# Second feed-forward part: another order of the 256 values within each matmul

## The chip, the cores and the metric

One core of a Trainium2 chip runs the whole kernel. The metric is the device time in microseconds (us) of one execution; lower is better.

## The reference

Two transformer blocks with D_MODEL 2048 on 256 tokens, in float32. Around the change, in the second block, the reference computes:

```python
def conv_gated_mlp(h, w_up, conv_w, conv_b, w_down):
    gate, up = jnp.split(h @ w_up, 2, axis=-1)
    return (jax.nn.gelu(dwconv_centred(gate, conv_w, conv_b), approximate=True) * up) @ w_down
...
        x = x + g2 * conv_gated_mlp(modulate(rmsnorm(x, norm2_g[l]), sh2, sc2), *ffn)
...
    return rmsnorm(x, final_norm_g)
```

w_up is 2048 x 11264 and w_down 5632 x 2048. What comes before (the first block, with attention, spatial gating and its own feed-forward; the modulation; the second block's attention, Fourier and long-convolution mixing) isn't touched by the change.

## The kernel before

**Chunks.** All weights go through TensorE in chunks of 512 x 512. A chunk c is loaded by SyncE's queue (1 MB, `load`, L347) into one of four buffers RAW, then split by halves into a high part WH (ScalarE, L519) and a rest WL (VectorE, L981), each with two buffers. The activations are split the same way into high and low (XH, XL; HH, HL). TensorE forms high x high, high x low and low x high, so a float32 product takes three matmuls in the format fp32r. The 400 chunks in which the weights are the stationary operand go through `ws` (L1786): per chunk 4 blocks kk of 128 rows x 4 blocks f of 128 columns x 3 products = 48 matmuls on line 1791. Each has a 128x128 block of weights as stationary operand and one activation tile of 128 partitions x 256 tokens as moving operand, and adds to `out[:, f, :]`, 256 columns of PSUM (two f share a bank of 512). A few earlier chunks go through `tok` (L1796), where the weights are the moving operand, 512 columns wide (L1802, L1804, L1805).

**Steps of the second feed-forward.** There are STEPS2 = 11 steps of 512 hidden columns. The part begins with 8 chunks (gate and up of step 0, numbers C_FF2 to C_FF2 + 7). Then `ff2_step(j)` (L2191) for j = 0 to 9, 12 chunks each: the gate of step j + 1 (4 chunks, `wide`), its up (4, `wide`), and the down product of step j (4, `down`). The last 4 chunks are the down product of step 10. Together 132 chunks. `wide` reads 16 tiles of XH and XL, `down` 4 tiles of HH and HL. In SBUF a tile is 1024 bytes per partition. With the base of 16512 bytes (L161), XH, XL, HH and HL begin at a multiple of 64 bytes; the first two tiles of XH are kept apart as XH_FIRST (L178, `tile_of` L207), which begins 32 bytes past a multiple of 64. In a `wide` of 4 chunks the first chunk reads XH_FIRST in 16 of its 48 matmuls.

**The engines beside it.** VectorE and ScalarE do, beside the splitting, the depthwise convolution (L1697 to L1707), gelu, the gating (L1715), the split of the hidden tile (L937, L1353) and the addition to X (L1720). Each engine's order is written out by hand and is the same for every step; they are tied by semaphores. TensorE waits for each half chunk's WH and WL (`high_ready`, `low_ready`), and for a free accumulator (`use`); two accumulators of two banks each take turns. After the last chunk come the last addition, the root of the mean square, the final norm and the output.

**Where the code decides.** `ws` is called from `product` (L1808), which passes the chunk's place c; in this part c.base is a constant for every chunk, since the steps are written out and not looped.

Of the kernel before, what the change touches and what calls it, by code (L numbers as in the profile page):

```python
# [8 lines left out]
P = 128  # L9
# [35 lines left out]
STEP1, STEP2 = 2 * SLOTS, 3 * SLOTS  # L45
# [9 lines left out]
C_FF2 = C_OUT2 + 4 * SLOTS  # L55
# [100 lines left out]
def build_program(nc, d, out):  # L156
# [6 lines left out]
    with ExitStack() as ctx:  # L163
# [126 lines left out]
        def acc_ws(s):  # L290
            return PS[:, 2 * s:2 * s + 2, :].rearrange("p b (h t) -> p (b h) t", t=T)
# [4 lines left out]
        def bank(n):  # L296
            return PS[:, n, :]
# [4 lines left out]
        def ctx_ws(n):  # L302
            return ctx_as(n).rearrange("p b (h t) -> p (b h) t", t=T)
# [42 lines left out]
        def _(sp):  # L346
# [77 lines left out]
            def ff1_step(j, first=False):  # L424

                c, _, a = ff1_place(j)
                order = Place(8 * j.base, j.i, 8 * j.per)
                for s in range(STEP1):
                    if s < SLOTS:
                        load(c.plus(s), cut(w_ff1, s, j.value(NB, NB)))  # L430
                    else:
                        load(c.plus(s), w_ff2[j.value()][:, :, (s - 4) * NB:(s - 3) * NB])
                    if s >= 2:
                        load_piece(a, s - 2, order.plus(s - 2))
                    elif not first:
                        load_piece(a.plus(-1), s + 6, order.plus(s - 2))
# [532 lines left out]
        def _(dve):  # L969
# [57 lines left out]
            def split_low(e, hi, lo, src, n):  # L1027
                dve.wait_ge(x_hi, 4 * e + n + 1)
                for (l4, k), (h4, _) in zip(parts_of(lo, n), parts_of(hi, n)):
                    ins = tt(l4, src[:, k, :], h4.bitcast(f32), ALU.subtract)  # L1030
                ins.then_inc(x_lo, 1)
# [740 lines left out]
        def _(pe):  # L1772
            MM = nc.tensor.matmul
# [7 lines left out]
            def use(q):  # L1781

                if q.since(2):
                    pe.wait_ge(acc_free[q.slot], q.turns(2))

            def ws(out, c, xh, xl, first, last, kk, low):  # L1786

                b = c.base % 2
                for n, (w, x) in enumerate(((WL, xh),) if low else ((WH, xh), (WH, xl))):
                    for f in (0, 2, 1, 3):  # L1790
                        ins = MM(out[:, f, :], w[:, b, kk, f * P:(f + 1) * P], x,  # L1791
                                 start=first and not low and n == 0 and f % 2 == 0, stop=last and low,
                                 skip_group_check=True)
                return ins
# [13 lines left out]
            def product(c, q, s, xh, xl, k0=0, first=True, last=True, fn=ws, out=None, e=None):  # L1808

                if q is not None and first:
                    use(q)
                early = s == 0 and e in WINDOWS
                if early:
                    pe.wait_ge(first_lo, WINDOWS.index(e) + 1)
                elif e is not None:
                    pe.wait_ge(x_lo, 4 * e + s + 1)
                if out is None:
                    out = (acc_ws if fn is ws else acc_as)(q.slot)
                for h in range(2):  # L1820
                    high_ready(c, h)
                    if h and early:
                        pe.wait_ge(x_lo, 4 * e + 1)
                    for low in (False, True):
                        if low:
                            low_ready(c, h)
                        for kk in range(HF * h, HF * h + HF):
                            ins = fn(out, c, tile_of(xh, k0 + kk), tile_of(xl, k0 + kk), first and kk == 0,
                                     last and kk == FT - 1, kk, low)
                    ins.then_inc(pe_half, 1)  # L1830

            def wide(c, q, s, fn=ws, e=None, xh=XH, xl=XL):

                product(c, q, s, xh, xl, 4 * s, s == 0, s == SLOTS - 1, fn, e=e)
# [92 lines left out]
            for c in range(C_OAB):  # L1927
                if c == 4:
                    pe.wait_ge(sm["mats_in"], 16)
                    norm_sum(N_IN, NT)  # L1930
                if T_SGU <= c < T_SGU + 8 and (c - T_SGU) % 2 == 0:
                    spatial_gating((c - T_SGU) // 2)
                if T_QK < c < T_QK + 16 and (c - T_QK) % 4 == 1:
                    head_sums((c - T_QK) // 4)
                for h in range(HEADS):
                    attention_step(h, c - T_ATT - S_ATT * h)
                first_columns(c)
                g, s = divmod(c, SLOTS)
                wide(Place(c), Place(g), s, tok if 4 <= g < 8 else ws,
                     {0: E_GAIN1, 2: E_NORM1}.get(g))  # L1940

            for n in range(4):
                for s in range(SLOTS):
                    c = Place(C_OAB + 4 * n + s)
# [3 lines left out]
                    if s == 2 and n >= 2:  # L1948
                        pe.wait_ge(sm["b_free"], n - 1)
                    product(c, Place(Q_OAB + n) if s < 2 else None, s, XH, XL, 4 * s, s % 2 == 0, s % 2 == 1,  # L1950
                            out=acc_ws((Q_OAB + n) % 2) if s < 2 else ctx_ws(n), e=E_OAB)
# [36 lines left out]
            c, q = Place(C_FF1_TAIL), Place(Q_FF1_TAIL)  # L1988
# [66 lines left out]
            for t in range(10 * SLOTS):  # L2055
                n, s = divmod(t, SLOTS)
# [31 lines left out]
            for n in range(FNG):  # L2088
# [3 lines left out]
                for m in range(2):  # L2092
                    ins = MM(bank(6 + n % 2)[:, 0:T], fcd[:, m, :], fU[:, n, m * T:(m + 1) * T],
                             start=m == 0, stop=m == 1)
# [212 lines left out]
```

## Time and profile before

| | us |
|---|---|
| median of 2 runs | 2567.72 (2567.47 to 2567.96) |
| the profiled execution | 2575.35 |
| its span, first to last instruction | 2573.6 |
| TensorE busy with matmuls | 2550.8 |
| VectorE busy | 1930.8 |
| ScalarE busy | 1140.4 |
| mean granted TensorE clock | 0.996 |

The rows below come from that one profiled execution. Matmuls are pipelined, so their durations overlap and a busy TensorE is not TensorE at its peak; the distance between starts tells the rate. PE is TensorE, PEld its weight load, DVE VectorE, ACT ScalarE, L1791 line 1791.

### The profile page before, as it was taken

What the parts mean: (1) busy time and instruction counts of PE and PEld (TensorE: products, weight loads), DVE (VectorE), ACT (ScalarE), POOL (GpSimd) and SP (SyncE); (2) the same over time, 40 slices, a digit from 0 to 9 for tenths busy, and PEclk for the clock granted to TensorE, in tenths of its full rate; (3) what the DMA queues carried; (4) which work ended last, traced back from release to release, by engine and by line L of the source; (5) the groups of instructions that cost most, each with busy time, mean ns of one, the idle gap of its engine ahead of it and who ended that gap; (6) DMA issues with size and microseconds to landing.
All of it is one profiled execution on the core that took longest, in us unless ns stands there. A gap on an engine that the chain in (4) does not pass through costs nothing.

```text
span 2573.6 us, 49600 instructions
## 1 busy us (share of the span) xinstructions
PE 2550.8 (99%) x20808; PEld 2468.6 (96%) x20808; DVE 1930.8 (75%) x2468; ACT 1140.4 (44%) x1225; POOL 0.2 (0%) x4
## 2 busy tenths in 40 slices
PE   9999999999999999999999999999999999999998
PEld 9889999999999999999999899959999999999998
DVE  8978887997999888888893237777766666666667
ACT  6556554444544444444442234333444444444443
POOL 0000000000000000000000000000000000000000
PEclk9999999999999999999999999989999999999999
DMA  8766767767888888888863254424555555555553
GB/s 312 259 238 214 241 230 249 249 240 247 289 285 286 290 283 285 287 284 284 280 234 104 94 180 148 143 76 152 169 190 196 197 192 190 193 196 197 190 190 113
DMA packets 282441, 558.10 MB, mean 217 GB/s; under 512 B 10295, under 2 KB 16728, under 8 KB 281944
## 3 DMA queue, kind: packets, MB, share of 16 engines
q1 hardware_dynamic: 282120, 553.47, 64.1%
q8 instruction: 133, 2.18, 0.3%
q10 hardware_dynamic: 144, 2.10, 0.2%
q14 instruction: 44, 0.36, 0.0%
HBM read 553.43 MB, written 2.10 MB: 216 GB/s over the span
## 4 chain that ended last, share of the span: by engine, by line
PE 93%; DVE 4%; DMA 1%; issue 1%; ACT 1%; SPq 0%; DVEq 0%; ACTq 0%
PE PS L1791 80%; PE PS L1805 3%; PE PS L1802 3%; PE PS L1804 3%; DVE WL L981 1%; PE PS L2123 1%; DMA w3h<-in_hy_w 1%; DMA adab<-in_ada_w 0%; PE PS L2038 0%; DMA X<-in_x 0%; PE PS L2112 0%; PE PS L1869 0%; DVE ada1c L1240 0%; DVE SQ L1007 0%; PE PS L2133 0%
## 5 line engine op out<-in xcount | busy, mean ns | idle before, releaser
L519 ACT ACTIVATE WH<-RAW 128x1024 fp32r<-128x1024 f32 x840 | 889.3, 1061 | 1278.2 <-PE PS L1791 1151.6
L981 DVE TENSOR_TENSOR WL<-RAW,WH 128x1024 fp32r<-128x1024 f32 x840 | 1018.1, 1223 | 579.7 <-ACT WH L519 570.6
L1791 PE MATMUL PS<-XL,WH 128*128 128x256 f32 x4288 | 664.2, 277 | 0.0
L1791 PE MATMUL PS<-XH,WH 128*128 128x256 f32 x3752 | 585.9, 278 | 1.6 <-ACT WH L519 0.9
L1791 PEld LDWEIGHTS PS<-XL,WH 128*128 128x128 f32 x4288 | 569.1, 188 | 0.0
L1791 PE MATMUL PS<-XH,WL 128*128 128x256 f32 x3752 | 503.2, 276 | 0.0
L1791 PEld LDWEIGHTS PS<-XH,WH 128*128 128x128 f32 x3752 | 498.2, 188 | 3.9 <-issue 2.3
L1791 PEld LDWEIGHTS PS<-XH,WL 128*128 128x128 f32 x3752 | 461.5, 188 | 0.0
L1791 PE MATMUL PS<-HH,WH 128*128 128x256 f32 x1728 | 268.0, 277 | 1.5 <-DVE X L1359 1.5
L1791 PE MATMUL PS<-HL,WH 128*128 128x256 f32 x1728 | 266.2, 276 | 0.0
L1791 PE MATMUL PS<-HH,WL 128*128 128x256 f32 x1728 | 231.1, 276 | 0.0
L1791 PEld LDWEIGHTS PS<-HH,WH 128*128 128x128 f32 x1728 | 228.3, 188 | 2.0 <-DVE X L1359 1.9
L1791 PEld LDWEIGHTS PS<-HL,WH 128*128 128x128 f32 x1728 | 228.0, 188 | 0.0
L1791 PEld LDWEIGHTS PS<-HH,WL 128*128 128x128 f32 x1728 | 212.0, 188 | 0.0
L1240 DVE SCALAR_TENSOR_TENSOR ada1c<-ada1b,ctmp,ada1c 128x512 f32<-128x512 f32 x240 | 164.3, 746 | 0.1
L1398 DVE SCALAR_TENSOR_TENSOR adac<-adab,ctmp,adac 128x512 f32<-128x512 f32 x224 | 157.3, 745 | 1.6 <-DMA adab<-in_ada_w 1.5
L1805 PE MATMUL PS<-WH,XL 128*128 128x512 f32 x224 | 87.9, 392 | 0.0
L1791 PE MATMUL PS<-XH_FIRST,WH 128*128 128x256 f32 x536 | 86.1, 283 | 0.0
L1359 DVE TENSOR_TENSOR X<-PS,X 128x1024 f32<-128x1024 f32 x64 | 77.9, 1217 | 0.0
L1804 PE MATMUL PS<-WH,XH 128*128 128x512 f32 x196 | 77.8, 397 | 0.0
L1791 PE MATMUL PS<-XH_FIRST,WL 128*128 128x256 f32 x536 | 73.6, 280 | 0.0
L1720 DVE SCALAR_TENSOR_TENSOR X<-PS,mod,X 128x256 f32<-128x256 f32 x176 | 72.7, 476 | 0.0
(278 smaller groups left out, 1848.4 us busy)
## 6 DMA issues: line engine op xcount, KB each, us to landing
RAW<-in_w_ff SPq DMA_DIRECT2D x128, 1024.0 KB, 6.2
RAW<-in_w_in SPq DMA_DIRECT2D x111, 1024.0 KB, 5.2
RAW<-in_w_up SPq DMA_DIRECT2D x88, 1024.0 KB, 5.0
adab<-in_ada_w SPq DMA_DIRECT2D x128, 512.0 KB, 5.4
RAW<-in_w_down SPq DMA_DIRECT2D x44, 1024.0 KB, 5.0
ada1b<-in_ada_w SPq DMA_DIRECT2D x64, 512.0 KB, 6.1
RAW<-in_w_out SPq DMA_DIRECT2D x32, 1024.0 KB, 5.1
RAW<-in_w_oa SPq DMA_DIRECT2D x8, 1024.0 KB, 5.2
```

The costliest lines, as they stand in the source:

```text
L519: A(WH[:, c.base % 2, hs], RAW[:, c.base % SLOTS, hs], ACT.Copy).then_inc(hi_done, 1)
L981: tt(WL[:, b, hs], RAW[:, c.base % SLOTS, hs], WH[:, b, hs].bitcast(f32), ALU.subtract)\
L1240: stt(acc, w, x, acc, ALU.mult, ALU.add)
L1359: tt(quarter(X, s), acc_ws(q.slot), quarter(X, s), ALU.add).then_inc(acc_free[q.slot], 1)
L1398: ins = ts(acc, w, x, None, ALU.mult) if n == 0 else stt(acc, w, x, acc, ALU.mult, ALU.add)
L1720: ins = stt(X[:, 4 * s + k, :], acc_ws(q.slot)[:, k, :], mod[:, 5 * KC + 4 * s + k, 0:1], X[:, 4 * s + k, :], ALU.mult, ALU.add)
L1791: ins = MM(out[:, f, :], w[:, b, kk, f * P:(f + 1) * P], x, start=first and not low and n == 0 and f % 2 == 0, stop=last and low, skip_gro ...
L1802: ins = MM(out[:, t, :], h, WL[:, b, kk, :], start=False, stop=last)
L1804: MM(out[:, t, :], h, WH[:, b, kk, :], start=first, stop=False)
L1805: ins = MM(out[:, t, :], l, WH[:, b, kk, :], start=False, stop=False)
L2123: ins = MM(bank(n % 2), Ef[:, 5 * t + m, :], hSD[:, o, 1 if m in (2, 3) else 0, t, :], start=t == 0, stop=t == 1)
```

## The change

`ws` passes both its output and its moving operand through `walked`, which gives the same 256 values in another order, as one access pattern with three dimensions. n is the number of the 12-chunk group, counted from the first chunk of the part; for chunks ahead of the part n is negative and the order stays plain, and so it does for n = 0 and n = 10. Group n begins at the up of step n: 4 up chunks and the 4 down chunks of `ff2_step(n - 1)`, then the 4 gate chunks of `ff2_step(n)`.

```diff
+            LINES = [(), ("t", 2, 16), ("h", 2, 16), ("t", 2, 32), ("h", 2, 2), ("t", 2, 2),
+                     ("t", 2, 8), ("t", 4, 16), ("h", 4, 16), ("h", 2, 4), ()]
+
+            def walked(x, c):
+
+                n = (c.base - C_FF2) // STEP2
+                if n < 0 or not LINES[n]:
+                    return x
+                kind, b, w = LINES[n]
+                if kind == "r":
+                    return x.rearrange("p (a w) -> p a w", w=w)[:, ::-1, :]
+                if kind == "t":
+                    return x.rearrange("p (a b w) -> p b a w", b=b, w=w)
+                return x.rearrange("p (b a w) -> p a b w", b=b, w=w)
+
             def ws(out, c, xh, xl, first, last, kk, low):
...
-                        ins = MM(out[:, f, :], w[:, b, kk, f * P:(f + 1) * P], x,
+                        ins = MM(walked(out[:, f, :], c), w[:, b, kk, f * P:(f + 1) * P], walked(x, c),
                                  start=first and not low and n == 0 and f % 2 == 0, stop=last and low,
                                  skip_group_check=True)
```

"t", b, w: pieces of w values; first every b-th piece from piece 0, then every b-th from piece 1, and so on. With ("t", 2, 16): values 0 to 15, 32 to 47, ..., then 16 to 31, 48 to 63, .... "h", b, w: the tile is cut in b parts, and pieces of w values are taken from the parts in turn. With ("h", 2, 2): values 0, 1, 128, 129, 2, 3, 130, 131, .... A value has 4 bytes, so a piece of 16 is 64 bytes and one of 2 is 8 bytes. Kind "r" isn't used.

## Rows read from the trace of the kernel before

**Rows 1.** The page: span, TensorE's share, the chain by engine and line.

```profile
span 2573.6 us, 49600 instructions
...
PE 2550.8 (99%) x20808; PEld 2468.6 (96%) x20808; DVE 1930.8 (75%) x2468; ACT 1140.4 (44%) x1225; POOL 0.2 (0%) x4
...
PE 93%; DVE 4%; DMA 1%; issue 1%; ACT 1%; SPq 0%; DVEq 0%; ACTq 0%
PE PS L1791 80%; PE PS L1805 3%; PE PS L1802 3%; PE PS L1804 3%; DVE WL L981 1%; PE PS L2123 1%; DMA w3h<-in_hy_w 1%; DMA adab<-in_ada_w 0%; PE PS L2038 0%; DMA X<-in_x 0%; PE PS L2112 0%; PE PS L1869 0%; DVE ada1c L1240 0%; DVE SQ L1007 0%
```

**Rows 2.** The nine changed groups by window: busy us, count, clock, DMA share.

```profile
core 0: us, PE busy (x) PEld busy (x) DVE busy (x) ACT busy (x) POOL busy (x), PEclk, DMA share, GB/s
1903.98:1969.49 65.51, 65.51 (x579) 65.51 (x577) 42.40 (x55) 28.30 (x27) 0.00 (x0) 1.00 0.58 193
...
2428.04:2493.54 65.50, 65.50 (x578) 65.50 (x577) 42.40 (x55) 28.30 (x27) 0.00 (x0) 1.00 0.59 194
sum 589.56, PE 589.56 PEld 589.56 DVE 381.65 ACT 254.73 POOL 0.00; mean PE 65.51 PEld 65.51 DVE 42.41 ACT 28.30 POOL 0.00
```

**Rows 3.** The chain of waits within the nine groups.

```profile
by line: PE PS L1791 100.0%
...
1903.92 589.67 PE PS L1791 x5185
```

**Rows 4.** All waits in the nine groups: waiting <- waited for: us, times, longest.

```profile
ACT WH L519 <- PE PS L1791: 334.8, 216, 1.8
DVE WL L981 <- ACT WH L519: 205.5, 153, 1.6
```

**Rows 5.** Groups of instructions by shape within the nine groups.

```profile
L1791 PE MATMUL PS<-XL,WH 128*128 128x256 f32 x1152 | 178.0, 277 | 0.0
...
L1791 PEld LDWEIGHTS PS<-XL,WH 128*128 128x128 f32 x1152 | 152.5, 188 | 0.0
...
L1791 PE MATMUL PS<-HH,WH 128*128 128x256 f32 x576 | 88.7, 276 | 0.0
...
L1791 PE MATMUL PS<-XH_FIRST,WH 128*128 128x256 f32 x144 | 22.7, 280 | 0.0
```

**Rows 6.** Timeline of TensorE over one down chunk (start us, us, what, xcount).

```profile
1996.80 0.62 PE L1791 MATMUL PS<-HH,WH 128*128 128x256 f32 x4
...
2002.24 0.62 PE L1791 MATMUL PS<-HH,WH 128*128 128x256 f32 x4
```

**Rows 7.** Timeline of TensorE, matmuls 512 columns wide.

```profile
133.17 0.39 PE L1804 MATMUL PS<-WH,XH 128*128 128x512 f32 x1
...
135.91 0.39 PE L1804 MATMUL PS<-WH,XH 128*128 128x512 f32 x1
```

**Rows 8.** Timeline of TensorE, a chunk that begins with XH_FIRST.

```profile
2493.54 0.63 PE L1791 MATMUL PS<-XH_FIRST,WH 128*128 128x256 f32 x4
...
2496.36 0.63 PE L1791 MATMUL PS<-XH,WH 128*128 128x256 f32 x4
2496.83 0.62 PE L1791 MATMUL PS<-XL,WH 128*128 128x256 f32 x4
...
2499.09 0.62 PE L1791 MATMUL PS<-XH,WH 128*128 128x256 f32 x4
```

**Rows 9.** Timeline of TensorE, a chunk with XH_FIRST in the slower gait.

```profile
465.08 0.63 PE L1791 MATMUL PS<-XH_FIRST,WH 128*128 128x256 f32 x4
465.55 0.63 PE L1791 MATMUL PS<-XL,WH 128*128 128x256 f32 x4
...
467.89 0.63 PE L1791 MATMUL PS<-XH,WH 128*128 128x256 f32 x4
...
470.72 0.63 PE L1791 MATMUL PS<-XH,WH 128*128 128x256 f32 x4
```

**Rows 10.** Timeline of TensorE, matmuls of plain 4-byte numbers.

```profile
1832.67 5.34 PE L1922 MATMUL PS<-mats 128*128 128x256 f32 x24
1837.66 0.58 PE L1791 MATMUL PS<-XH_FIRST,WH 128*128 128x256 f32 x2
```

## The prediction

> **What bounds the kernel now.** I read the shares and the chain first. TensorE is busy for 2550.8 of 2573.6 us and the chain of waits that ended last lies on it for 93%, 80% on line 1791 alone, which is the line that changes [rows 1]. Then I cut the part of the second feed-forward where another order applies into its nine groups of 12 chunks. A group is 12 chunks x 48 matmuls = 576; the nine are 5184 matmuls and take 589.56 us, 65.51 us each, at a granted clock of 1.00, the upper level of 2.4 GHz [rows 2]. In this stretch the chain is one piece of line 1791 [rows 3], and nobody makes TensorE wait: the waits are ScalarE's for TensorE (334.8 us) and VectorE's for ScalarE (205.5 us) [rows 4]. VectorE works 42.41 and ScalarE 28.30 us of each 65.51, the transfers have a share of 0.58 [rows 2]. So the time of this stretch is the number of matmuls times the spacing of their starts, and a slower matmul has no cover at all: each nanosecond on each of the 5184 is 5.18 us of the total.
>
> **The spacing.** A matmul's row says 276 ns [rows 5], but they overlap; the starts tell the rate. Down chunks: from 1996.80 to 2002.24 us, 48 matmuls, 5.44 us, 113.3 ns each [rows 6]. 256 columns at 2.4 GHz are 106.7 ns, 256 cycles; 113.3 ns are 272 cycles, 16 too many, which is one for each 16 values or 64 bytes of the tile read. The matmuls 512 columns wide, 12 of them from 133.17 to 135.91 us, start 228 ns apart [rows 7], so the extra goes with the columns and isn't a fixed cost of an instruction. Whether reading, writing or the weight load (188 ns in its rows, overlapped [rows 5]) makes it, no row tells.
>
> **The change part by part.** No instruction, wait, buffer or transfer is added, removed or moved. What changes is the order in which one matmul walks its 256 values: it reads x in pieces and writes the sums in the same pieces, so value t still goes to place t. Accumulation over the matmuls is as before. Chunks 0 to 11 and 120 to 131 of the part keep the plain order; nine groups get the orders of LINES. Per matmul I count two things. Breaks in the run of addresses: 16, 16, 8, 128, 128, 32, 16, 16, 64 for groups 1 to 9, together 424. And changes of the 64-byte piece being read (the plain order has 16): 16, 16, 16, 128, 32, 32, 16, 16, 64, together 336, which is 192 more than the 144 of nine plain orders. (XH_FIRST lies 32 bytes off, so that its pieces of 16 and 32 straddle one boundary more; that is 32 matmuls of a group's 576 and left out of the counts.)
>
> *Reading.* The trace of before has no broken order, so I bound it by the nearest rows. From below: the spacing can't go under 106.7 ns; if a new order took all extra cycles away, 5184 x 6.7 ns = 34.6 us would go. Nothing tells that a detour over other pieces would remove a cycle per 64 bytes, and the weight load beside it may want the same time. From above: the nearest row in which a matmul's reading lies otherwise on the addresses is XH_FIRST, which by its offset begins 32 bytes off the 64-byte grid, while XH, XL, HH and HL begin on it. Its matmuls stand at 280 ns beside 276 [rows 5], and the chunk that has 16 of them takes from 2493.54 to 2499.09, 5.55 us [rows 8], 0.11 us more than a plain one. That is 7 ns for each misaligned matmul, some 17 cycles, and such a matmul touches 17 pieces instead of 16. One reading of this is that each touched piece costs its full 17 cycles however little of it is used; then groups with 2, 4 or 8 values per piece would pay 192 x 7.08 ns x 576 = 783 us. The rows speak against it: in the stretch from 465.08 us all matmuls start 117.7 ns apart, aligned or not; 24 with the 16 misaligned ones take 465.08 to 467.89 (2.81 us), the next 24, all aligned, 467.89 to 470.72 (2.83 us) [rows 9]. Four misaligned ones there take 0.47 us (465.08 to 465.55), 117.5 ns each, while 17 x 17 cycles would be 120.4. And after the misaligned ones of 2493.54 the first aligned four still go at 117.5 (2496.36 to 2496.83) [rows 8]: it is a slower gait of the engine, which something small sets off. I take this as the price of a disturbance: 4.4 ns x 5184 = 23 us if all of the changed matmuls fell into it. 
>
> *Writing.* The same breaks hit the accumulation. The nearest rows for an engine at a slower rate are those of line 1922, 256 columns of plain 4-byte numbers: 24 of them from 1832.67 to 1837.66, 0.208 us each [rows 10], about two cycles per column. That is the price if every write (or read) went alone. I take nothing here too, by the same reason.
>
> The Trainium skill says two things of this. Its page "Advanced Engine Details and Errata", section Memory Cachelines, says that every two consecutive values in PSUM should be contiguous for best throughput, and that a 16-byte line of SBUF wants at least two hits; all nine orders keep both, and by it the sum stays at nothing. The same section and "PSUM — Partial Sum Buffer", section Specifications (TRN2), also say that any non-contiguous pattern in PSUM slows matmuls significantly; by that all nine groups would be slow, which is the third rival below. No row of this trace shows either, as none has a broken pattern.
>
> *The engines beside it.* If the spacing grows, VectorE and ScalarE, which have 23.1 and 37.2 us to spare in each group [rows 2], get more, and the loads more time. Nothing new can become late. After the last chunk the tail is untouched.
>
> **The sum.** Profiled execution: 2575.35 us, its span 2573.6. The changed stretch stays at 589.56 us, all others stay. The median of the runs is 7.6 us under the profiled one, so I apply differences to the median: 2567.72 + 0 = 2567.7. A measurement of this kernel tells about 2%, 51.4 us, from no change: 9.9 ns on each changed matmul.
>
> **The rivals.**
> 1. *The cycle per 64 bytes is a cycle per change of piece.* For: 16 extra cycles for 16 pieces, 32 for the wide ones [rows 6, 7]. Against: it may as well be a beat of time. Price: 192 x 0.417 ns = 80 ns over the nine orders, x 576 = 46 us: 2613.8. It shows in h 2 2 (+47 ns), h 2 4 (+20), t 2 2 and t 2 8 (+7 each).
> 2. *Slower: every break of the run costs.* Place: TensorE's walk over addresses, on line 1791 in groups 1 to 9. With one cycle of 2.4 GHz per break: 424 x 0.417 ns x 576 = 101.8 us: 2669.5. With two (one at 1.2 GHz): 203.6 us: 2771.3. For: there is no cover, and two of the nine orders break every 2 values. Against: nothing but that pairs may be the unit. It decides (over 2%) from 0.21 ns per break. A doubling of only the two groups of 2 values, 2 x 65.5 = 131 us, 2698.7, lies within it.
> 3. *Every broken pattern goes at the rate of one value at a time.* 208 - 113.7 = 94 ns x 5184 = 489 us: 3057. For: the engine has such a rate [rows 10], and one mechanism, writes that are gathered only along an unbroken run, would put all nine orders on it. Against: a pair is whole in every order, and those rows are of another number format, which by itself may be the cause. (This is the form that the Trainium skill's "PSUM — Partial Sum Buffer", section Specifications (TRN2), gives to the matter; no row here bears it out.)
> 4. *The detour saves the extra cycles*: up to 34.6 us less: 2533.
>
> **How the numbers follow.** No effect, or one within a disturbance of the gait: 0.50. Rival 1: 0.12. Rival 2: 0.27. Rival 3: 0.08. Rival 4: 0.03. The likeliest gives 2567.7, its own range 2550 (half of rival 4) to 2591 (all at 117.7 ns). The range reaches to rivals 1 and 2: 2545 to 2771; rival 3, the whole of 4 and still dearer breaks stay out, some 0.15. Slower by over 2%: rivals 2 and 3 and the upper quarter of rival 1, 0.38. Faster by over 2% could come only with more than rival 4 gives: 0.01. Within 2%: 0.61.
>
> **What would show it.** Right: all nine groups still take 65.5 us, chunks without XH_FIRST 5.44 us. Rival 1: only groups 4, 5, 6 and 9 grow, and 4 far more than 5, though both break every two values. Rival 2: groups 4 and 5 grow alike, by 31 us or more, and the groups of 16 values by 4 us. Rival 3: all nine at about 120 us. If ScalarE's waits for TensorE grow by what the groups grow, the time is TensorE's own; if TensorE shows waits before line 1791, my reading that nobody holds it was wrong. The prediction is wrong if pieces of 2 or 4 values alone cost more than 51 us.

## The result and the profile after

The changed kernel takes 2693.59 us (median of 2 runs, 2692.77 to 2694.41) against 2567.72; the ratio on record is 1.0488, 95% interval 1.0471 to 1.0505. It is slower by 125.9 us. That is inside the range of the prediction and not what it called likeliest.

The page of the changed kernel, which answers to [rows 1]; line 1806 is now the matmul of `ws`:

```profile
span 2691.0 us, 49600 instructions
...
PE 2669.6 (99%) x20808; PEld 2579.3 (96%) x20808; DVE 1931.9 (72%) x2468; ACT 1140.5 (42%) x1225; POOL 0.2 (0%) x4
...
PE 93%; DVE 4%; DMA 1%; issue 1%; ACT 1%; SPq 0%; DVEq 0%; ACTq 0%
```

The count of instructions is the same and so is the work of VectorE and ScalarE; only TensorE, with its weight load, is busy for longer. The two spans, 2691.0 and 2573.6 us, differ by only 117.4 us because the profiled execution of before had lost 8.5 us ahead of the part: its first chunk starts at 1837.66 us, that of the changed kernel at 1829.18. Its granted clock was 0.92 from 1650 to 1700 us and 0.94 from 1700 to 1750, where the changed kernel had 1.00. Here are the nine groups by window, as in [rows 2] (length and busy us of each engine, then the granted clock, the share of the transfers and GB/s):

```profile
1895.81:1965.70 69.89, 69.89 (x579) 69.89 (x578) 42.52 (x55) 28.23 (x27) 0.00 (x0) 1.00 0.56 183
1965.70:2034.86 69.16, 69.16 (x578) 69.16 (x577) 42.50 (x55) 28.32 (x27) 0.00 (x0) 1.00 0.55 183
2034.86:2104.00 69.14, 69.14 (x579) 69.14 (x578) 42.50 (x55) 28.28 (x27) 0.00 (x0) 1.00 0.56 183
2104.00:2198.77 94.77, 94.77 (x579) 94.77 (x578) 42.59 (x55) 28.20 (x27) 0.00 (x0) 1.00 0.43 139
2198.77:2330.84 132.07, 132.07 (x577) 119.68 (x577) 42.59 (x55) 28.19 (x27) 0.00 (x0) 1.00 0.29 96
2330.84:2399.86 69.02, 69.02 (x577) 69.02 (x576) 42.52 (x55) 28.29 (x27) 0.00 (x0) 1.00 0.54 177
2399.86:2468.90 69.04, 69.04 (x579) 69.04 (x577) 42.51 (x55) 28.26 (x27) 0.00 (x0) 1.00 0.55 183
2468.90:2537.93 69.03, 69.03 (x579) 69.03 (x578) 42.52 (x55) 28.25 (x27) 0.00 (x0) 1.00 0.55 184
2537.93:2610.95 73.02, 73.02 (x578) 73.02 (x577) 42.51 (x55) 28.84 (x27) 0.00 (x0) 1.00 0.53 176
sum 715.14, PE 715.14 PEld 702.75 DVE 382.76 ACT 254.86 POOL 0.00; mean PE 79.46 PEld 78.08 DVE 42.53 ACT 28.32 POOL 0.00
```

715.14 less 589.56 of before is 125.6 us: the whole difference lies in the nine groups. Divided by 576, one matmul costs, against 113.7 ns before:

| group, order | ns | us over before |
|---|---|---|
| 1: t 2 16 | 121.3 | 4.4 |
| 2: h 2 16 | 120.1 | 3.7 |
| 3: t 2 32 | 120.0 | 3.6 |
| 4: h 2 2 | 164.5 | 29.3 |
| 5: t 2 2 | 229.3 | 66.6 |
| 6: t 2 8 | 119.8 | 3.5 |
| 7: t 4 16 | 119.9 | 3.5 |
| 8: h 4 16 | 119.8 | 3.5 |
| 9: h 2 4 | 126.8 | 7.5 |

The two orders of 2 values hold 95.9 us, three quarters. The waits and the chain in these groups (they answer to [rows 3, 4]):

```profile
ACT WH L519 <- PE PS L1806: 460.0, 216, 4.5
DVE WL L981 <- ACT WH L519: 327.5, 181, 4.3
```
```profile
1895.75 715.24 PE PS L1806 x5185
```

ScalarE's wait for TensorE grew by 125.2 us, from 334.8 to 460.0, as much as the groups; TensorE still waits for nobody. In group 5 the starts of four matmuls are 0.92 us apart, where it was 0.45:

```profile
2250.12 1.10 PE L1806 MATMUL PS<-HH,WH 128*128 128x256 f32 x4
2251.04 1.10 PE L1806 MATMUL PS<-HL,WH 128*128 128x256 f32 x4
```

So the time is TensorE's own. What the profile doesn't tell is which side of a matmul it is: the reading of the tile from SBUF, or the adding in PSUM.

### The profile page after: what moved, and what is told of

It reads as the page before. It is cut to its first block, busy times and chain, and to the rows that moved or that the text cites. A ratio compares the mean times of both kernels' runs of the same rounds, so it can differ in the third digit from the quotient of the medians.

```text
span 2691.0 us, 49600 instructions
## 1 busy us (share of the span) xinstructions
PE 2669.6 (99%) x20808; PEld 2579.3 (96%) x20808; DVE 1931.9 (72%) x2468; ACT 1140.5 (42%) x1225; POOL 0.2 (0%) x4
## 4 chain that ended last, share of the span: by engine, by line
PE 93%; DVE 4%; DMA 1%; issue 1%; ACT 1%; SPq 0%; DVEq 0%; ACTq 0%
PE PS L1806 81%; PE PS L1817 2%; PE PS L1820 2%; PE PS L1819 2%; DVE WL L981 1%; PE PS L2138 1%; DMA w3h<-in_hy_w 0%; PE PS L2053 0%; DMA X<-in_x 0%; DVE ada1c L1240 0%; DVE X L1359 0%; PE PS L1884 0%; DVE SQ L1007 0%; DVE NT L1023 0%; PE PS L2148 0%
## 5 line engine op out<-in xcount | busy, mean ns | idle before, releaser
L1806 PE MATMUL PS<-XL,WH 128*128 128x256 f32 x4288 | 692.7, 284 | 0.0
L1806 PE MATMUL PS<-XH,WH 128*128 128x256 f32 x3752 | 611.0, 285 | 2.4 <-ACT WH L519 1.5
L1806 PEld LDWEIGHTS PS<-XL,WH 128*128 128x128 f32 x4288 | 588.9, 189 | 2.8
L1806 PE MATMUL PS<-XH,WL 128*128 128x256 f32 x3752 | 528.3, 284 | 0.0
L1806 PEld LDWEIGHTS PS<-XH,WH 128*128 128x128 f32 x3752 | 515.8, 189 | 7.1 <-issue 2.9
L1806 PEld LDWEIGHTS PS<-XH,WL 128*128 128x128 f32 x3752 | 481.6, 189 | 2.4
L1806 PE MATMUL PS<-HH,WH 128*128 128x256 f32 x1728 | 282.6, 286 | 0.3 <-DVE X L1359 0.3
L1806 PE MATMUL PS<-HL,WH 128*128 128x256 f32 x1728 | 280.8, 285 | 0.0
L1806 PE MATMUL PS<-HH,WL 128*128 128x256 f32 x1728 | 245.5, 285 | 0.0
L1806 PEld LDWEIGHTS PS<-HL,WH 128*128 128x128 f32 x1728 | 238.3, 189 | 1.4
L1240 DVE SCALAR_TENSOR_TENSOR ada1c<-ada1b,ctmp,ada1c 128x512 f32<-128x512 f32 x240 | 164.5, 748 | 0.1
L1806 PEld LDWEIGHTS PS<-XH_FIRST,WH 128*128 128x128 f32 x536 | 74.6, 189 | 0.6
```

The source lines that it names most:

```text
L1240: stt(acc, w, x, acc, ALU.mult, ALU.add)
L1806: ins = MM(walked(out[:, f, :], c), w[:, b, kk, f * P:(f + 1) * P], walked(x, c), start=first and not low and n == 0 and f % 2 == 0, stop= ...
```

## The experiments

In all of them a group is one of the nine, 576 matmuls long, and a window of one divided by 576 is the spacing. Groups are named by number and order.

Seven of the runs (reads alone, writes alone, more orders, single values, shifted starts, wider matmuls, the weights' addresses) are one execution each; what they tell is read from their windows, in which a group with the same code repeats within 0.05 us from run to run, but for the slower gait told of below. `order` is `walked` with its table given from outside, and g is the number of the group. All diffs are against the kernel before.

**Reads alone, writes alone.** Two kernels with the nine orders on one operand, READS or WRITES, and the plain order on the other:

```diff
-                        ins = MM(out[:, f, :], w[:, b, kk, f * P:(f + 1) * P], x,
+                        ins = MM(order(out[:, f, :], WRITES[g]), w[:, b, kk, f * P:(f + 1) * P], order(x, READS[g]),
```

> The reads follow the nine orders, the writes keep the plain order, so each matmul adds the token columns to other places than it should: the output of the second feed-forward is shuffled, the amount of work is the same. In the changed kernel the spacing of the starts per group was 121.3, 120.0, 120.0, 164.4, 229.3, 120.0, 120.0, 120.0, 126.7 ns (plain 113.3). Theory R (the reading of the tile from SBUF is the limit): all nine spacings as in the changed kernel within 1 ns, time about 2693 us. Theory W (the writing to PSUM is the limit): all nine at 113.3 ns plus the 0.4 ns of XH_FIRST, time about 2568 us. Theory B (the constant step to 120 ns comes from one side, the growth with pieces of 2 and 4 values from the other): groups 4, 5 and 9 differ from the changed kernel and the six others don't, or the other way round.

> The writes follow the nine orders, the reads keep the plain order (the output of the second feed-forward is shuffled, the work is the same). Theory R (reading is the limit): all groups at 113.7 ns, time about 2568 us. Theory W (writing is the limit): spacings 121.3, 120.0, 120.0, 164.4, 229.3, 120.0, 120.0, 120.0, 126.7 ns, time about 2693 us. Theory B (each side has a share): what is missing in the run with the reads alone stands here.

Measured: 2696.1 us with the reads alone, 2568.5 us with the writes alone, beside 2567.4 for the kernel before. Windows of groups 1, 4, 5 and 9 of the first (busy us of TensorE, clock, share of transfers, GB/s):

```profile
1899.16:1969.04 69.88, 69.88 (x578) 1.00 0.56 184
...
2107.34:2202.11 94.77, 94.77 (x578) 1.00 0.41 139
2202.11:2334.19 132.08, 132.08 (x579) 1.00 0.29 96
...
2541.27:2614.30 73.03, 73.03 (x579) 1.00 0.53 175
```

and groups 4 and 5 of the second:

```profile
2093.65:2159.15 65.50, 65.50 (x578) 1.00 0.58 193
2159.15:2224.66 65.51, 65.51 (x579) 1.00 0.58 193
```

This is theory R: all of the cost is in the reading, to 0.01 us per group. Beside a reading at 113.7 ns none shows in the writing, not even with pairs from two halves of the block. The 2.5 us by which the reads alone are over the changed kernel lie ahead of the groups: group 1 begins at 1899.16 instead of 1895.81.

**Without the two orders of 2 values.** Groups 4 and 5 plain, the rest as in the change:

```diff
+            READS = [(), ("t", 2, 16), ("h", 2, 16), ("t", 2, 32), (), (), ("t", 2, 8), ("t", 4, 16), ("h", 4, 16), ("h", 2, 4), ()]
+            WRITES = [(), ("t", 2, 16), ("h", 2, 16), ("t", 2, 32), (), (), ("t", 2, 8), ("t", 4, 16), ("h", 4, 16), ("h", 2, 4), ()]
```

> The change without the two orders of 2 values (groups 4 and 5 are plain, the seven others as in the change). By the groups of the changed kernel these two hold 29.3 and 66.6 us of the 125.5 us, so if the groups are independent and TensorE alone sets the time: 2693.6 - 95.9 = 2597.7 us, 1.2% over the kernel before. Rival: the cost is one of the clock or of a wait that the slow groups hand on to later ones; then groups 6 and 9 change too and the time is off by more than 5 us.

Measured: 2597.97 us, ratio to before 1.0119 (1.0103 to 1.0134). The costs of the groups add up, but for one detail. Groups 4 and 5, both plain now:

```profile
2105.21:2172.30 67.09, 67.09 (x579) 1.00 0.57 186
2172.30:2237.80 65.50, 65.50 (x578) 1.00 0.59 194
```

Group 4 takes 1.6 us more than the same code in group 5. It is in a slower gait, a spacing of some 117.8 ns that lasts over many matmuls, which the prediction had seen near 465 us [rows 9]. Group 4 cut at the second of its two chunks that begin with XH_FIRST:

```profile
2105.21:2150.43 45.22, 45.22 (x387) 1.00 0.57 186
2150.43:2153.71 3.28, 3.28 (x30) 1.00 0.44 166
2153.71:2172.30 18.59, 18.59 (x167) 1.00 0.60 191
```

The first 8 chunks, after the broken order of group 3, take 117.8 ns per matmul (45.22 us for 384), though the first of them begins with XH_FIRST; the 28 matmuls from 2150.43 take 117.1; the rest, 164 matmuls, 113.4.

**XH_FIRST on the grid of 64 bytes, and off it at another place.** The kernel before with one offset changed:

```diff
-        XH_FIRST = at("XH_FIRST", [P, 2, T], 80 * K + 32, f32r)
+        XH_FIRST = at("XH_FIRST", [P, 2, T], 80 * K + 64, f32r)
```

> The kernel before, with XH_FIRST moved from 32 to 64 bytes past its old origin, so that it begins on a multiple of 64 bytes; plain order everywhere. If the 0.11 us that each chunk with XH_FIRST costs comes from its place: these chunks take 5.44 us instead of 5.55 in the two feed-forwards (36 of them and about 12 elsewhere), 48 x 0.113 = 5.4 us less, 2562 us. If it comes from something else at the start of a wide product (a semaphore wait, the change of the accumulator): 5.55 us as before and no difference.

Measured: 2624.82 us, ratio 1.0222 (1.0209 to 1.0236), so both sides of the expectation were wrong. The first of its nine groups, all of which take 67.82 or 67.83 us (117.8 ns per matmul):

```profile
1931.23:1999.06 67.83, 67.83 (x579) 1.00 0.56 186
```

With 96 instead of 64:

> The kernel before with XH_FIRST 96 bytes past its origin instead of 32: again 32 bytes off the grid of 64, but at another place. The run with XH_FIRST on the grid was 57 us slower, with all matmuls at 117.8 ns instead of 113.3. Theory G (a tile that begins off the grid pushes reading and weight loading back into the faster of two gaits): as before, 2567 us, 113.3 ns in most chunks. Theory A (the distance between addresses decides by itself, the grid has no part): some other share of slow chunks, a time anywhere between 2567 and 2625 us.

Measured: 2566.55 us, ratio 0.9993 (0.9983 to 1.0003), groups at 65.52 us. This agrees with theory G, as far as three places can tell: two tiles off the grid, which I had read as a small loss (0.11 us per chunk, [rows 8]), keep most of the kernel in the faster gait; on the grid the nine groups go at 117.8 ns. They hold 21 of the 57 us; some 34 lie ahead of group 1, which begins at 1931.23 us instead of 1896.90 (run with more orders). That a chunk with XH_FIRST ends the slower gait is seen in group 4 of the run without the two orders of 2 values, at 2153.71 us, but not each of them does: the one at 2105.21 there didn't, and neither did the one at 465.08 us in the kernel before [rows 9]. What decides it stays open.

**More orders.** Both operands in one order again, WRITES with the same table as READS:

```diff
+            READS = [(), ("t", 2, 64), ("h", 2, 64), ("h", 2, 32), ("t", 2, 4), ("t", 4, 2), ("h", 4, 2), ("t", 8, 2), ("t", 4, 4), ("h", 2, 8), ()]
```

> Nine other orders, for reads and writes, in groups 1 to 9: t 2 64, h 2 64, h 2 32, t 2 4, t 4 2, h 4 2, t 8 2, t 4 4, h 2 8. Theory L: the reader fetches 16 bytes at a time (four values) and one such fetch costs 4.25 to 4.75 cycles of 2.4 GHz, whatever part of it is used. Plain: 64 fetches, 113.3 ns. So t 2 64, h 2 64, h 2 32, h 2 8: 120 ns; t 2 4 and t 4 4: 120 to 127 ns; t 4 2 and t 8 2: 128 fetches, 229 ns as t 2 2; h 4 2 like h 2 2 if a fetch is kept for a moment, else 229. Theory N: the price of t 2 2 comes from going to the next neighbour; with pairs 32 or 64 bytes apart (t 4 2, t 8 2) it falls to the 164 ns of h 2 2 or less. Theory C: the price is one per break (424 breaks of the change); then t 2 64 and h 2 64 with 4 breaks stand at 113 to 115 ns, not 120.

Measured: 113.7, 113.7, 118.8, 117.8, 233.3, 223.4, 219.9, 114.5, 123.3 ns. Windows of groups 1, 4, 5, 7 and 8:

```profile
1896.90:1962.41 65.51, 65.51 (x579) 1.00 0.58 193
...
2096.36:2164.21 67.85, 67.85 (x579) 1.00 0.56 187
2164.21:2298.57 134.36, 134.36 (x578) 1.00 0.30 98
...
2427.25:2553.91 126.66, 126.66 (x578) 1.00 0.30 100
2553.91:2619.84 65.93, 65.93 (x577) 1.00 0.56 183
```

Pairs 32 or 64 bytes apart (t 4 2, t 8 2) and pairs from four parts in turn (h 4 2) cost about the double as well, so theory N falls. Theory L was right on the pairs, but wanted 120 ns for pieces of 64 and got 113.7. Pieces of 4 with 64 breaks cost 114.5 ns and pieces of 64 nothing, so the price isn't one per break either, though t 2 64 came out as theory C had it. And a pattern of three dimensions by itself is free.

**Single values, and more writes.**

```diff
+            READS = [(), ("t", 2, 1), ("t", 4, 1), ("h", 2, 1), ("t", 16, 1), ("t", 16, 2), ("t", 16, 4), (), (), (), ()]
+            WRITES = [(), (), (), (), (), (), (), ("t", 16, 2), ("h", 16, 2), ("h", 16, 4), ()]
```

> Groups 1 to 6 read t 2 1, t 4 1, h 2 1, t 16 1, t 16 2, t 16 4 and write plainly; groups 7 to 9 read plainly and write t 16 2, h 16 2, h 16 4 (so the output of the second feed-forward is shuffled, the work is the same). Theory L (a fetch of 16 bytes costs 4.25 to 4.75 cycles): t 2 1 has two values of each fetch, 229 ns; t 4 1 and t 16 1 one value, 256 fetches, about 459 ns; t 16 2 229 ns; t 16 4 about 127 ns; h 2 1 alternates between two lines and shows whether two fetches are kept: 120 to 130 ns if so, 459 if not. Rival (two hits in a 16-byte line are enough, the slow orders suffer from something else): t 2 1 at 113 to 120 ns. Writes: 113.7 ns in groups 7 to 9 if the writing order is free for pieces of two values or more; 120 ns or more if strides of 64 bytes matter there.

Measured: 229.3, 233.3, 111.7, 220.0, 228.4, 135.3 ns, then 113.7 three times for the writes. Groups 1 to 3:

```profile
1897.29:2029.36 132.07, 132.07 (x578) 1.00 0.30 101
2029.36:2163.76 134.40, 134.40 (x578) 1.00 0.28 94
2163.76:2228.09 64.33, 64.33 (x577) 1.00 0.57 186
```

Theory L falls: t 4 1 takes one value from each 16 bytes and should have cost 459 ns, it costs 233, no more than two values from each. And h 2 1, which breaks after every single value, is the fastest of all, faster than plain. What both have in common becomes visible if the order is cut in twos and the first and the second place of each two are followed apart (the even and the odd places). In h 2 1 the even places read 0, 1, 2, 3 and the odd ones 128, 129, 130, 131, each staying in its line of 16 bytes for four values. In t 2 1, t 2 2, t 4 1 and t 16 2 each stream changes its line with every value. In pieces of 4 on a line's start it has two values per line. This is theory S, put to the test next. The three orders of the writes are free too; writes of single values were not run, so nothing tells what they cost.

**Shifted starts.** Each matmul reads 256 values from an offset within two tiles:

```diff
+                    read = two.rearrange("p k t -> p (k t)")[:, kind[0]:kind[0] + T]
+                    if len(kind) > 1:
+                        read = order(read, *kind[1:])
```

> Groups 1 to 9 read 256 values that begin 2, 4, 8, 12 values after the start of an even tile (plain order), then from 2 on as t 2 4, from 2 on as t 2 8, then from 0 on as h 4 1 and h 8 1, and from 8 on as h 2 1; writes plain, the products are not the right ones, the amount is. Theory S: the reader takes the values by twos, the even and the odd places of the order each from a 16-byte line that serves only as long as the next value of that stream lies in it; a line that serves one place alone costs double, one that serves two is free. So pieces of 4 at a distance of 2 values from the line's start (t 2 4 from 2) cut each line in one pair each: 220 to 233 ns, while the same order from 0 took 117.8; t 2 8 from 2: between the two, about 170 ns; h 4 1: its even places alternate between two lines like h 2 2: 150 to 230 ns; h 8 1: 220 to 233; h 2 1 from 8: 111.7. Rival P (what counts is the length of the piece, 4 or more is nearly free wherever it begins): t 2 4 and t 2 8 from 2 at 114 to 127 ns. The plain order from 2, 4, 8, 12: all 113 to 120 ns in both; those off the grid of 64 bytes (all four are) at 117 to 120 if being off the grid is what costs XH_FIRST its time.

Measured: 120.0, 116.8, 118.3, 117.3 ns for the plain order from 2, 4, 8, 12. Then t 2 4 from 2: 229.9. t 2 8 from 2: 166.7. h 4 1: 143.3. h 8 1: 220.1. h 2 1 from 8: 111.7. Groups 5 to 9:

```profile
2171.00:2303.43 132.43, 132.43 (x579) 1.00 0.30 100
2303.43:2399.47 96.04, 96.04 (x577) 1.00 0.40 132
2399.47:2482.01 82.54, 82.54 (x578) 1.00 0.46 153
2482.01:2608.80 126.79, 126.79 (x578) 1.00 0.30 100
2608.80:2673.14 64.34, 64.34 (x578) 1.00 0.57 187
```

The same pieces of four cost 117.8 ns from 0 and 229.9 from 2. This tells the two theories apart: it isn't the length of the piece but how it lies on the lines of 16 bytes. t 2 8 from 2 has pairs alone in their line for two of its four twos, and costs half of the doubling, as worked out ahead. h 4 1 at 143 ns is a little under its bound. There and in h 2 2 (164.5) each stream alternates between two lines and pays a part of the doubling; where it goes through four lines in turn (h 8 1, 220.1; h 4 2, 223.4) it pays nearly the whole, which theory S as it stands doesn't explain. In every order that was run the even and the odd places change their line at the same twos, so whether the two streams really count apart, or a two of places counts as one access, isn't told.

**Wider matmuls, patterns that only go upward.** Groups 1 to 5 read two tiles with 512 columns, groups 6 to 9 every other piece of two tiles:

```diff
+                            read = order(two, *kind[1:]) if len(kind) > 1 else two
+                            write = out[:, f:f + 2, :].rearrange("p f t -> p (f t)")
+                        else:
+                            read = two.rearrange("p (a b w) -> p b a w", b=2, w=kind[1])[:, k % 2]
```

> The products of groups 1 to 9 are not the right ones here, the amount read and added is. Groups 1 to 5: matmuls of 512 columns that read two tiles in one and write two blocks (half as many matmuls): plain, t 2 16, t 2 2, h 2 2, h 2 4. Groups 6 to 9: 256 columns, every other piece of 128, 16, 4, 2 values out of two tiles, a pattern of two dimensions that goes upward only; writes plain. If the extra goes with the columns: 226.7, 240, 459, 329, 253 ns for the 512-wide ones, and it is the reading; if the step from 113.3 to 120 is a fixed cost of an instruction with a broken pattern: t 2 16 at 233 ns. If it is the weight load (128 columns, the same for either width) that holds the spacing at 113.3: plain at 213 to 220 ns. Groups 6 to 9: if any break brings the step, 120 ns already for half 128 (one break), else 113.3; half 16: 120; half 4: 120 to 127; half 2: 128 fetches of 16 bytes, 229 ns.

Measured, per matmul of 512 columns (288 to a group): 233.1, 238.3, 453.3, 326.7, 252.3 ns. Half 128, 16, 4, 2: 116.5, 121.7, 117.5, 229.9 ns. Groups 1, 3, 4 and 9:

```profile
1899.64:1966.76 67.12, 67.12 (x291) 1.00 0.57 188
...
2035.40:2165.95 130.55, 130.55 (x289) 1.00 0.30 100
2165.95:2260.05 94.10, 94.10 (x290) 1.00 0.41 134
...
2537.61:2670.02 132.41, 132.41 (x579) 1.00 0.30 100
```

The dear orders double with the columns though the weight load is the same 128 columns, so it is the tile's reading that makes them. The plain 512 columns stand at 233.1 ns and not at the 213 to 220 of a spacing that the weight load holds. Of the patterns that only go upward, half 2 came out as expected (229.9) and half 4 below its 120 to 127. Half 128 came out between the two values that were named: part of that group goes in the faster gait, the larger part in the slower.

**The weights' addresses.** The tile plain in groups 1 to 6 and t 2 16 in 7 to 9:

```diff
+                            o = f // 2 * P + WEIGHTS[g][0]
+                            block = w[:, b, kk, o:o + P]
+                            if len(WEIGHTS[g]) > 1:
+                                block = w[:, b, kk, 0:P * WEIGHTS[g][1]:WEIGHTS[g][1]]
```

> The tile is read in plain order in groups 1 to 6 and as t 2 16 in 7 to 9; what changes is the block of weights that each matmul loads (so the products are not the right ones, the amount is the same): from 0, 4, 8, 16 values past a block's start in groups 1 to 4, every second and every fourth value in groups 5 and 6, from 0, 8, 16 in groups 7 to 9. Theory I (the small differences, 113.3 against 117.8 in plain order and the step to 120 with pieces of 8 to 32, come from tile reading and weight loading meeting in the same memory, so they hang on how their addresses lie to each other): the groups 1 to 4 differ by 1 ns or more among themselves, and so do 7 to 9; groups 5 and 6, where the weights come from two and four times as many lines, go slower by several ns or more. Theory T (the tile's own reading makes them all): 113.3 (or 117.8 where the engine is in its slower gait) in groups 1 to 6 and 121.3 as before in 7 to 9, whatever the weights do.

Measured: 113.7, 118.6, 117.5, 118.6 ns with the weights from 0, 4, 8, 16; 120.1 and 233.3 with every second and every fourth value; 121.3, 120.1, 120.1 for t 2 16. Groups 1, 2 and 6:

```profile
1895.73:1961.24 65.51, 65.51 (x578) 1.00 0.58 193
1961.24:2029.55 68.31, 68.31 (x579) 1.00 0.57 187
...
2234.70:2369.10 134.40, 134.40 (x579) 1.00 0.30 98
```

Theory I's condition is met: with the same tile in the same order, 16 bytes more in the weights' address cost 4.9 ns, and groups 7 to 9 differ by 1.2. So the weights' address bears on the small differences; that the two meet in the same memory is only argued. A weight load with one value per 16 bytes brings the spacing to 233.3 ns beside a plain tile.

**A version that beats both.** h 2 1 on the reads of the second feed-forward, with plain writes; the sums then stand in another order of tokens, and their three readers put them back (the gating, in four instructions instead of one, is left out here):

```diff
+                                 x.rearrange("p (b a) -> p a b", b=2) if c.base >= C_FF2 and c.i is None else x,
...
+                A(GS[:, :, :].rearrange("p k (b a) -> p k a b", b=2),
+                  acc_ws(q.slot).rearrange("p k (a b) -> p k a b", b=2), ACT.Copy).then_inc(acc_free[q.slot], 1)
...
+                    xs = X[:, 4 * s + k, :].rearrange("p (b a) -> p a b", b=2)
+                    ins = stt(xs, acc_ws(q.slot)[:, k, :].rearrange("p (a b) -> p a b", b=2),
```

> The kernel before; in the 132 chunks of the second feed-forward the tile is read as h 2 1 (value 0, 128, 1, 129, ...), the writes are plain, and the three places that read the sums (the copy of the gate, the gating, the addition to X) put them back with the same order of their own tiles. In an earlier run h 2 1 stood at 111.7 ns against 113.3, also in the chunks with XH_FIRST (5.36 us against 5.44 and 5.55). If this holds and TensorE alone sets the time: 132 x 0.08 + 22 x 0.11 = 13 us less than before, 2554 us, 0.5%. Rival: VectorE and ScalarE go slower over tiles in that order (up to twice) and the last additions, which nothing hides, take it back: 2560 to 2568 us.

Measured: 2556.81 us beside 2568.06, ratio 0.9957 (0.9943 to 0.9970). A group of it, and the addition to X (durations in ns, min, median, max):

```profile
1895.04:1959.36 64.32, 64.32 (x578) 1.00 0.60 197
```
```profile
L1726 DVE SCALAR_TENSOR_TENSOR X<-PS,mod,X x176: 646/668/698, 1924.3 to 2542.2; 128x256 f32<-128x256 f32 x176
```

Every chunk takes 5.36 us, those with XH_FIRST too, so the 11 groups of the part save 1.19 us each, 13.1 us. The kernel gained 11.2, between the expectation and its rival. The additions went from a median of 476 ns in the kernel before (L1720) to 668; inside the steps TensorE hides them. Behind the last matmul of the part the profiled execution (2558.11 us) takes 3.4 us more than before. The chains of the two kernels, before first, and the windows of TensorE's last matmuls in the same order:

```profile
2555.84 1.58 DVE X L1720 x4
...
2560.76 2.01 PE PS L1869 x8
```
```profile
2536.22 2.10 DVE X L1726 x4
...
2541.83 3.68 PE PS L1876 x8
```
```profile
2560.76:2562.76 2.00, 1.99 (x8) 1.00 0.00 0
```
```profile
2541.83:2545.50 3.67, 3.66 (x8) 0.54 0.00 0
```

The 13 additions on the chain take 1.7 us more. The other 1.7 us go with the clock: those eight matmuls got 0.54, near the lower level of 1.2 GHz, where the kernel before had 1.00, after TensorE had stood idle for 1.97 and 0.33 us in waiting for VectorE and ScalarE (0.38 us before).

## Why the prediction was right or wrong

What bounds the kernel: right. The chain, the waits, the unchanged 42.5 and 28.3 us of the other engines and the sum of the groups (125.6 of 125.9 us) all say that each nanosecond of a matmul in the nine groups goes into the time, uncovered.

"The value I take for the likeliest case is nothing, since pieces of at least two values, always on an 8-byte boundary, leave each access as wide as two values": this is the step that failed, the term *Reading* of the sum, put at nothing and measured as 125.6 us. The access may be two values wide, but one such access isn't enough for a line of 16 bytes. The runs show that a pair alone in its line costs two times the time (t 2 2, 229.3 ns, and t 2 4 from 2, 229.9), while a whole aligned line of four values costs 1 to 13 ns more than plain (114.5 to 126.8; 22 more at a distance of 256 bytes, 135.3). 95.9 us come from the two orders of pairs; the other 29.7 come from the seven groups of longer pieces, whose mechanism stays open. The Trainium skill's "Advanced Engine Details and Errata", section Memory Cachelines, asks for two hits on a 16-byte line; I counted values. Counted as two successive accesses of two places each, the rule agrees with every order at about the double here, for this format at 2.4 GHz, but it doesn't give the prices between (h 2 2, h 4 1); counted in values it is refuted by t 2 1 and t 2 2, which have two values of each line and stand at 229.3 ns.

The writing: right to take nothing, and measured as nothing (2568.5 us). The Trainium skill's "PSUM — Partial Sum Buffer", section Specifications (TRN2), has any non-contiguous pattern in PSUM slow matmuls significantly; the trace of the writes alone, 65.50 us per group for pieces of 2 to 32, doesn't agree. I gave that rival 0.08. The reason given, whole pairs, is not tested for the writes, as no run writes single values.

Rival 1 (one cycle per change of 64-byte piece) put h 2 2 far above t 2 2, and it is the other way round: 164 against 229. (Its 32 extra cycles for the wide matmuls are a misreading too: 228.3 less 213.3 ns are 36.) Rival 2 gave the sign and the size (101.8 us for one cycle per break) but its mechanism is wrong: it wanted 53 ns on both orders of two, where 51 and 116 came, and 3 ns on t 2 32, where 6 came; t 4 4, with 64 breaks, costs 1 ns. The doubling of the two groups, 131 us, named inside rival 2, was the nearest: they cost 95.9. So the range holds the result by luck, through a rival whose mechanism the runs refute. The reason I had against rival 2 ("pairs may be the unit") was the very error.

The argument against a full price for each touched 64 bytes held: t 2 8 and h 2 4 didn't go up to 227 or 453 ns. The reading of XH_FIRST as a disturbance that sets off a slower gait was half right. The 0.11 us are not 7 ns on each of 16 misaligned matmuls: from 2493.54 to 2496.83 us 28 matmuls, aligned ones among them, stand 117.5 ns apart [rows 8]. The gait is real, but it isn't all of the step to 120 in the six groups of long pieces: they cost 22.2 us, and six groups at the prediction's 4.4 ns would be 15. What I had not seen is that XH_FIRST off the grid also keeps most of the kernel out of the slower gait, as the run with it on the grid shows, which is slower by 57 us.

The choice between no effect at 0.50 and slower at 0.38 rested on no row, since the trace has no broken pattern; the weight came from a rule of two read in the kindest way. What makes the 16 extra cycles of the plain order, and why h 2 2 and h 4 1 pay 51 and 30 ns where t 2 2 pays 116 and h 8 1 106, stays open. That the small differences hang on the weights' address as well as on the tile's is shown, by which distances isn't.

## What to carry to other kernels

For a kernel that TensorE bounds as here, count the moving operand's order in lines of 16 bytes and accesses of two 4-byte values: the moving tile of an fp32r matmul should take four neighbouring values on a 16-byte boundary, or let even and odd places run through one line each; a pair alone in its line doubled the matmul. The order of the writes to PSUM, in pieces of two values or more, was free, so a layout can be changed there rather than in the read. When matmuls stand at a spacing that is a few per cent off, try the address of an operand before the schedule: 32 bytes on one pair of tiles were worth 57 us here, and reading the two halves of a tile in turn gained 0.4%.

## What was not expected of the hardware

- The order h 2 1, a break after every value, is faster than plain: 111.7 ns against 113.3, and it stays there in chunks that hold a tile off the grid.
- The engine has two gaits for one and the same instruction stream, 113.3 and 117.8 ns, at a granted clock of 1.00 in both; one pair of tiles 32 or 96 bytes past its origin leaves most of the kernel in the first, 64 bytes most of it in the second.
- One value from each 16 bytes costs the moving tile no more than two (233.3 and 229.3 ns for 256 values), while a weight load with one value from each brings the spacing to 233.3 ns with only 128 columns.
